# A two-layer encoder's norms: rows scaled by their inverse roots before they are transposed, or afterwards

## What is computed

```python
def rms_norm(x, g):
    xf = x.astype(jnp.float32)
    y = xf * lax.rsqrt(jnp.mean(xf * xf, axis=-1, keepdims=True) + EPS)
    return (y * g.astype(jnp.float32)).astype(x.dtype)

for layer in (even, odd):
    h = h + mixer(rms_norm(h, ln_mix[layer]))
    h = h + cross_attention(rms_norm(h, ln_cross[layer]), rms_norm(mem, ln_mem[layer]))
    h = h + hier_moe(rms_norm(h, ln_ffn[layer]))
out = rms_norm(h, ln_final)
```

## Time and profile before

| | |
|---|---|
| runs | 1172.38, 1172.42, 1177.09 us; median 1172.42 |
| span of the profiled execution | 1166.6 us; its own time with what lies around the span is not listed, the three runs stand for it |
| TensorE busy | 1073.4 us, 92% |
| VectorE, ScalarE busy | 274.1 us, 177.2 us |
| DMA | 284.09 MB, mean 244 GB/s |

### The profile page before, as it was taken

The page is one execution under the profiler, slowest core; times in us unless marked ns, Lnnn a source line. Parts: engine busy times, 40 slices in busy tenths (PEclk is TensorE's granted clock), DMA queues, the critical chain, the costliest instruction groups (busy, mean ns, idle before and its releaser), DMA issues.

```text
span 1166.6 us, 11120 instructions
## 1 busy us (share of the span) xinstructions
PE 1073.4 (92%) x4580; PEld 649.5 (56%) x4580; DVE 274.1 (23%) x676; ACT 177.2 (15%) x368; POOL 11.1 (1%) x21
## 2 busy tenths in 40 slices
PE   5998798999999999899999999997988799999996
PEld 4577367454444443478867777785464544444432
DVE  4125232341111111402121212122134311111114
ACT  2105202031111110111111111111021211111101
POOL 1020000000000000000000000000000000000000
PEclk9999899999999999899999999998999799999998
DMA  9855034229999999983491770953051099999992
GB/s 335 311 157 200 17 144 158 77 73 411 425 426 428 425 429 428 280 246 75 90 249 26 177 188 2 281 192 139 1 217 66 7 399 424 429 427 426 429 429 99
DMA packets 108231, 284.09 MB, mean 244 GB/s; under 512 B 3719, under 2 KB 81623, under 8 KB 95897
## 3 DMA queue, kind: packets, MB, share of 16 engines
q1 hardware_dynamic: 106736, 279.72, 64.8%
q0 software_dynamic: 1168, 3.40, 1.1%
q10 hardware_dynamic: 280, 0.31, 0.1%
HBM read 282.31 MB, written 1.11 MB: 243 GB/s over the span
## 4 chain that ended last, share of the span: by engine, by line
PE 88%; DVE 5%; DMA 4%; issue 2%; ACT 1%; DVEq 0%; SPq 0%; ACTq 0%
PE banks L928 81%; PE banks L1244 4%; DMA ring<-expert_w_up_in 3%; PE banks L931 2%; ACT scratch L676 1%; DMA scratch<-mem_in 1%; DVE scratch L1904 0%; DVE tmp L1489 0%; DVE nrm L1592 0%; DVE mx L1584 0%; ACT nrm L725 0%; DVE rst L1491 0%; DVE h L1503 0%; DVE nrm L1531 0%; DVE nrm L1606 0%
## 5 line engine op out<-in xcount | busy, mean ns | idle before, releaser
L928 PE MATMUL banks<-ring,scratch 128*64 128x512 f32 (+1 forms) x1760 | 433.9, 594 | 12.6 <-DMA ring<-expert_w_up_in 5.4
L928 PEld LDWEIGHTS banks<-ring,scratch 128*64 128x64 f32 (+1 forms) x1760 | 162.2, 144 | 274.0 <-issue 270.9
L928 PE MATMUL banks<-nT,ring 128*128 128x256 f32 x1104 | 240.7, 379 | 0.6 <-DVE scratch L604 0.6
L928 PEld LDWEIGHTS banks<-nT,ring 128*128 128x128 f32 x1104 | 209.7, 190 | 29.0 <-issue 1.2
L928 PE MATMUL banks<-ring,nT 128*128 128x384 f32 (+2 forms) x352 | 116.6, 487 | 0.0
L928 PEld LDWEIGHTS banks<-ring,nT 128*128 128x128 f32 x352 | 64.0, 191 | 44.7 <-issue 14.3
L928 PE MATMUL banks<-scratch 128*128 128x256 f32 (+4 forms) x292 | 67.2, 416 | 14.1 <-ACT scratch L676 10.0
L676 ACT ACTIVATE scratch<-banks 128x512 f32<-128x512 f32 (+1 forms) x84 | 47.5, 585 | 202.5 <-PE banks L928 112.1
L928 PEld LDWEIGHTS banks<-scratch 128*128 128x128 f32 (+2 forms) x292 | 49.3, 196 | 30.9 <-ACT scratch L676 14.7
L1511 DVE TENSOR_TENSOR h<-banks,h 128x512 f32<-128x512 f32 x56 | 38.8, 692 | 117.3 <-PE banks L1244 117.3
L928 PE MATMUL banks<-scratch,nrm 128*128 128x256 f32 x256 | 61.7, 398 | 2.4 <-issue 2.4
(11 more groups left out here) (146 smaller groups left out, 440.6 us busy)
## 6 DMA issues: line engine op xcount, KB each, us to landing
ring<-expert_w_gate_in SPq DMA_DIRECT2D x32, 2048.0 KB, 13.2
ring<-expert_w_up_in SPq DMA_DIRECT2D x32, 2048.0 KB, 14.2
ring<-expert_w_down_in SPq DMA_DIRECT2D x32, 2048.0 KB, 11.6
ring<-odd_w_in_in SPq DMA_DIRECT2D x72, 512.0 KB, 7.2
ring<-xkv_w_in SPq DMA_DIRECT2D x4, 2048.0 KB, 12.5
ring<-even_w_in_in SPq DMA_DIRECT2D x3, 2048.0 KB, 20.9
scratch<-bias_rows SPq DMA_DIRECT2D x8, 576.0 KB, 7.8
ring<-even_w_out_in SPq DMA_DIRECT2D x2, 2048.0 KB, 10.2
```

Of the source, the lines that this page charges most:

```text
L928: return giving_back(nc.tensor.matmul(dst, lhsT, rhs, start=start, stop=stop))
```

## The change

Raw rows are transposed with the identity as soon as they are there, one pass a piece and with no wait for a root. The evacuation multiplies by the gain as before. The inverse roots are kept for all norms (roots) and enter where the results are read:

- as a number per token on the partitions: values of the memory (v0a to v1b, odd values), the scale of cross attention's exponentials and of the negated maxima (scaled, negated), the odd logits, and the router's logits;
- as a row over the free dimension, "spread": TensorE multiplies ones with the two diagonals into a bank (spread), VectorE copies it to SBUF (rbc, or rbc1 in norm 1). Memory keys and odd keys are multiplied by rbc at their evacuation; norm 1 multiplies all its chunks by rbc1 and the gain at once, on VectorE alone.

With it go: k0b and k1b move from ScalarE to VectorE (BY_DVE); odd pieces go by kind, 1 and 2 to VectorE, 0, 3 and 4 to ScalarE; TensorE waits for the copies of the bias rows (vec_sb) before norm 1's spread; in norms 2, 3, 5 and 6 VectorE works out tile 1's root after its evacuations.

```diff
+        SPREAD = {"m": 0, "1": 1, "4": 2}
+        SCALED = {"2": 0, "5": 1, "4": 2}
...
-        def norm_source_ready(eng, name):
+        def norm_source_ready(eng, name, t=0):
...
-                piece_in(eng, "nm1")
             else:
-                eng.wait_ge(resid, AFTER[name] + 2)
+                eng.wait_ge(resid, AFTER[name] + 2 + 2 * t)
...
-                if (k % 2 == 1) != is_act:
+                if (name != "1" and k % 2 == 1) != is_act:
...
+                        if name == "1":
+                            last = nc.vector.scalar_tensor_tensor(out=dst[:, c, :], in0=src, scalar=gain[:, c:c + 1],
+                                                                  in1=rbc1, op0=ALU.mult, op1=ALU.mult)
...
+        BY_DVE = {"k0a", "k0b", "k1a", "k1b"}
 
         def by_act(name):
-            return name in BY_ACT or PIECES[name] % 2 == 1
+            return name in BY_ACT or (name not in BY_DVE and PIECES[name] % 2 == 1)
...
+        def evacuate_keys(eng, is_act, name, dst):
+
+            if is_act:
+                return
+            piece_in(eng, name)
+            nc.vector.tensor_tensor(dst, pbank(name).rearrange("p (b s) -> p b s", b=2),
+                                    rbc.unsqueeze(1).to_broadcast([P, 2, SEQ]),
+                                    ALU.mult).then_inc(evac[PIECES[name] % 2], 1)
...
-            if (k % 2 == 1) != is_act:
+            kind = m % 5
+            if (kind not in (1, 2)) != is_act:
                 return
...
             elif kind == 2:
-                last = put(ok[:, 1:3].rearrange("p g s -> p (g s)"), b[:, :])
+                last = nc.vector.tensor_tensor(ok[:, 1:3], b.rearrange("p (b s) -> p b s", b=2),
+                                               rbc.unsqueeze(1).to_broadcast([P, 2, SEQ]), ALU.mult)
...
                 for t in range(2):
                     last = nc.scalar.activation(prob[:, n, t, :], bank[n][:, t * 256:(t + 1) * 256], ACT.Exp,
-                                                bias=negm[:, n, t:t + 1], scale=float(P) ** -0.5,
+                                                bias=negm[:, n, t:t + 1], scale=scaled[:, l, t:t + 1],
...
             def norm(name):
-                i = NORM_SEQ[name]
                 for t in range(TILES):
-                    pe.wait_ge(diag_set, 2 * i + 1 + t)
+                    norm_source_ready(pe, name, t)
...
-                            last = mm(b[:, at:at + P], NORMS[name][0][:, t, c * P:(c + 1) * P], diag[:, t, :], True, True)
+                            last = flip(b[:, at:at + P], NORMS[name][0][:, t, c * P:(c + 1) * P])
...
+            def spread(name):
+
+                pe.wait_ge(diag_set, SPREAD[name] + 1)
+                for t in range(TILES):
+                    last = mm(spread_bank(name)[:, t * P:(t + 1) * P], ones, diag[:, t, :], True, True)
+                last.then_inc(rbc_ps, 1)
...
+            pe.wait_ge(id_in, 16)
             norm("m")
             keys(0, 0, "m")
+            spread("m")
             keys(0, 1)
...
+            pe.wait_ge(vec_sb, 1)
+            spread("1")
             norm("1")
...
-            for m in range(5):
+            head_piece(0, 0, 0)
+            spread("4")
+            for m in range(1, 5):
                 head_piece(m, 0, 0)
...
+                if name == "m":
+                    squares(0)
+                    squares(1)
+                    evacuate_norm(dve, False, name)
+                    both_roots()
+                    dve.wait_ge(id_in, 16)
+                    on_diagonal()
+                    spread_out(rbc)
+                elif name == "1":
+                    squares(0)
+                    squares(1)
+                    both_roots()
+                    middle()
+                    on_diagonal()
+                    spread_out(rbc1)
+                    evacuate_norm(dve, False, name)
+                elif name == "4":
+                    dve.wait_ge(resid, at + 4)
+                    evacuate_norm(dve, False, name)
+                    squares(1)
+                    both_roots()
+                    on_diagonal()
+                    scores_scales()
+                    spread_out(rbc)
                 else:
                     add(at, 0)
                     add(at, 1)
                     dve.wait_ge(ssq_act, i + 1)
                     variance(0)
-                    step(rsqrt([0]))
-                    on_diagonal(0)
+                    step(rsqrt(rst, [0]))
                     for f in range(2):
                         add(at, 2 + f)
                         dve.wait_ge(resid, at + 3 + f)
                         squares(f)
-                    step(v.tensor_tensor(ssq[:, 1:2], ssq[:, 1:2], ssq[:, 2:3], ALU.add))
+                    evacuate_norm(dve, False, name)
+                    step(v.tensor_tensor(sums[:, 1:2], sums[:, 1:2], sums[:, 2:3], ALU.add))
                     variance(1)
-                    rsqrt([1]).then_inc(rstd_set, 1)
+                    rsqrt(rst, [1]).then_inc(rstd_set, 1)
                     dve.wait_ge(rstd_set, i + 1)
-                    on_diagonal(1)
+                    if name in SCALED:
+                        scores_scales()
...
-                v.tensor_scalar(negm[:, n, :], mx[:, n, :], -float(P) ** -0.5, None, ALU.mult).then_inc(maxed, 1)
+                v.tensor_tensor(negm[:, n, :], mx[:, n, :], negated[:, a // X_HEADS, :], ALU.mult).then_inc(maxed, 1)
...
+                for t in range(TILES):
+                    last = v.scalar_tensor_tensor(out=lg[:, t], in0=pbank(k)[:, t * NR:(t + 1) * NR],
+                                                  scalar=root("36"[l], t), in1=rb[:, l], op0=ALU.mult, op1=ALU.add)
```

More of the change, by code:

```diff
@@ L577, in evacuate_filler @@
                 i = "ab".index(name[2])
-                evacuate(eng, is_act, name, two(xkT[:, 1, 2 * i:2 * i + 2]))
+                evacuate_keys(eng, is_act, name, xkT[:, 1, 2 * i:2 * i + 2])
             elif name in ("v1a", "v1b"):
-                evacuate(eng, is_act, name, xv[:, 1, "ab".index(name[2]), :])
+                t = "ab".index(name[2])
+                evacuate(eng, is_act, name, xv[:, 1, t, :], scale=root("m", t))
         def evacuate_norm(eng, is_act, name):
@@ L698, in rows_for_gathers @@
                                                 src[:, t, :].rearrange("p (q c) -> p q c", c=CH), ACT.Copy,
-                                                scale=rst[:, t:t + 1])
+                                                scale=root(name, t))
                 middle()
@@ new lines, in scores_scales @@
+                def scores_scales():
+                    n = SCALED[name]
+                    step(v.tensor_scalar(scaled[:, n, :], rst, float(P) ** -0.5, None, ALU.mult))
+                    if n < DEPTH:
+                        step(v.tensor_scalar(negated[:, n, :], rst, -float(P) ** -0.5, None, ALU.mult))
+                if name == "7":
+                    dve.wait_ge(resid, at + 4)
+                    squares(1)
+                    both_roots()
+                    dve.wait_ge(lnf_in, 16)
+                    for t in range(TILES):
+                        for f in range(2):
+                            cols = slice(f * 512, (f + 1) * 512)
+                            v.scalar_tensor_tensor(out=rows(t)[:, cols], in0=src[:, t, cols], scalar=rst[:, t:t + 1],
+                                                   in1=lnf[:, cols], op0=ALU.mult, op1=ALU.mult).then_inc(fin_set, 1)
+                    return
```

114 lines of the change are left out of this document (62 added, 52 removed).

## The result

| | before | after |
|---|---|---|
| median of four runs (lowest, highest) | 1172.4 us (1170.78, 1177.09) | 1178.84 us (1178.09, 1182.49) |
| profiled execution: own time, span | span 1166.6 | 1182.49, 1180.6 |

The ratio is 1.006, with a 95% interval of 1.0031 to 1.0089. A second comparison (first experiment) gave 1.0035 [1.0018, 1.0053]. By the medians the change costs 6.4 and 3.9 us, 0.35 to 0.6%; the forecast was 1173.1 us, +0.65. The time lies in the range and in its upper part; the first median is even above 1178.3, where the prediction's own "slower" begins, to which it had given 0.21. What carried it there is the subject of the rest.

The account below looks back on a forecast made before the run. TensorE was taken as the bound, busy 92% of the span and carrying 88% of the chain. Gains at norms 2 to 6 against losses elsewhere, chiefly +10.15 in the odd layer, summed to +0.65: 1173.1 us, range 1167 to 1180.

Parts of the forecast that it names:

- Norm 4: After the experts: transposes start straight behind the projection without waiting for roots and diagonals, first odd product earlier; -7.75 us.
- The branch: TensorE's jump over its second expert pass, now between projection and transposes: between 0 and 4.54 us, taken as 0.
- Norms 5 and 6: TensorE no longer waits for tile 1's diagonal; tile 1 is turned earlier; -3.1 and -2.95 us.
- Norms 2 and 3: Fillers already hide the roots; half of tile 0's records and a little of tile 1 go; -1.05 and -1.2 us.
- The memory norm: At the start: rows turned earlier, but key weights limit the gain and key products run on a cold clock; +1.0 us.
- Norm 1: TensorE waits for bias-row copies, diagonals and spread (+1.7), then value products run at half rate (+2.15); +3.8 us.
- the row that tells how TensorE recovers is the last odd head: Clock still 0.50 up to 818 us after transposes from 809.73, so 4.3 us of value products charged at half rate, +2.15.
- Cross attention 0: In layer 0, VectorE evacuates the second key filler ahead of normalising head 0, delaying its transposes; +1.75 us.
- The odd layer: Normalising waits for VectorE's piece 2 in all seven heads with a next head, not three; 4 x 2.54, +10.15 us.
- Rival A: Slower: the clock falls at three or four of norms 2, 4, 5 and 6; 1179.7 or 1181.9 us; chance 0.21.
- Rival B: Faster: odd-head normalising is ready in time, the 10.15 go, 1163 us; with unpaid cold stretches 1166.6 or less, chance 0.12.
- Rival C: A raw-row transpose takes as long as the diagonal pair; norms 2 to 6 give back about 3 us, 1176; chance 0.06.

Follow-up runs that it names:

- first experiment: The changed kernel with no edit, measured in more runs and profiled a second time: 1176.31 us (nine runs), ratio 1.0035 to the kernel before.
- again: The second profile of the unedited changed kernel, taken in the first experiment, whose median was 1176.31 us.
- the identity products: The changed kernel with norm transposes made as ordinary products with the identity: in all norms 1186.84 us, in norms m, 1, 2 and 3 only 1181.98 us.
- before with the order mended: The kernel before with VectorE normalising a head ahead of piece 2 of the next one, nothing else: 1166.52 us, 0.9932.
- the kernel with the order mended: The changed kernel with VectorE normalising a head ahead of piece 2 of the next one: 1158.18 us, 0.9878.

## Why the prediction came out as it did

**Norm 4, -7.75: right.** -8.11 to the first odd product, forecast -8.2 (the 0.45 of the spread is in the next segment). The branch, taken as 0 between 0 and 4.54, was 0 in the change by its place in the program; two variants with the same norm 4 paid 1.75 and 2.36 us there. That was luck: the reason given, that queued products cover it, held there as well.

**Norms 5 and 6, -3.1 and -2.95: right.** -3.12 and -2.87 in the profile after (-3.13 and -2.88 in "again"), and 0.5 us lost behind the second router.

**Norms 2 and 3, -1.05 and -1.2: right at the norms.** The records ahead of norm 2 come 9.12 us later than before, its first product 8.07 later; from cross attention 0 to the router it is -0.92 and -0.94. But the stretch behind that router takes 1.6 to 3.3 us longer in the change and in nearly all variants, with a clock of 0.50. The sum has no term for it. The version with 22 transposes in the wait for key weights had 10.60 there, like before; the three profiles of kernels with before's norms had 10.67 or 10.68. What decides it stays open: not transposes as such, as the identity products show.

**The memory norm, +1.0: right in kind, and it varies.** +1.7 and +0.5 in the two profiles of the change (start of keys -1.56 and -1.48, key products +3.28 and +1.97). The row on the cold norm is misread: 21 records in 4 us are 0.19 us each, two thirds of the rate of the earlier trace rows and not half.

**Norm 1, +3.8: mis-sized.** The way to the value product grew by 2.28, forecast 1.7. The value products, charged with 2.15 at half rate, lost 0.65 and 0.08: in the profile after the clock is 0.58 from 59.6 to 61.0 us and 1.00 from there on. So 2.4 to 2.9. The step that failed is "the row that tells how TensorE recovers is the last odd head": there it stood 6.25 us before it made transposes, here 3.05 us before four records of products and sixteen transposes, and the clock was back at 61.0 us, 5.9 us after TensorE went on at 55.15; behind the last odd head it was still 0.50 at 818, 8.3 us after 809.73. Nor is that row fixed: the twelve records of products behind the last head took 5.49 us in the profile of before and 2.86 with the clock at 1.00 in three other profiles, one of them of before with the order mended.

**Cross attention 0, +1.75: right**, 1.75 and 1.74. The three terms that it names add up to 1.47; where the rest comes from it doesn't say.

**The odd layer, +10.15: right in kind, too small by 2 to 5.** It was 12.9 and 15.8 with the spread's 0.45. Seven long heads came, by the mechanism and the 2.5 us named. What was missing: the wait is long enough for the clock to fall in some of them, and after the seventh that costs 1.3 in both profiles. The scale from memory, taken at 0 to 0.3 in the last head, fits: TensorE waits 6.38 us there instead of 6.25. The prediction used "waits of 2.05 and 2.37 us are today followed by full rate" from two single rows; three such waits in one execution can't say how seven will do.

**Rival A** foresaw the loss by clock but in the wrong places. Behind norms 2, 4 and 5 and in the first 3 us behind norm 6 the profile after shows a clock of 1.00; the falls were in the odd heads' waits and at the router, and transposes hold the clock up. Its figure, 1179.7, is nearer to the first median than the forecast is; the mechanism at the norms is not what gave it. **Rival B** is refuted by the change, and is nearly the kernel with the order mended. **Rival C** falls: 16 transposes take 2.04 us at norm 4, 0.13 each, and a piece as a diagonal product takes 2.05/8 = 0.26.

So the sum of +0.65 moves up by clock falls in the odd layer (2.3 to 5.2) and at the router (1.6 to 3.3) and down by some 1.2 at norm 1: +3.3 to +8, around the measured 3.9 and 6.4. That it came out so near zero at first is the cancelling of 16 us won against 17 lost, and a miss of 5 in the odd layer shows in full. The first expert stage, from its gathering products (246.75 us before, 258.92 after) to the end of its projection, has no term in the sum. It took 238.5 us before, 238.9 after and 242.1 in "again"; 1.7 of the last is a fall at those first products (8.83 us instead of 7.14). What the rest is stays open.

## What to carry to other kernels

When a change redistributes work among engines, write out each receiving engine's program and look for what now stands ahead of the thing the bottleneck waits for: one line cost 11.8 us, another order of the same instructions won 18.1. Compare a profile with the spread of its runs before taking differences of spans. In this kernel a wait of 2.3 us on TensorE cost its length and, in two to four of seven, 1.0 to 1.7 us more behind it. Where a change and its side effects come together, as inverse roots and pieces by kind here, cost them separately: the idea was worth 6 to 8 us (2 to 11 by the intervals), the assignment that came with it -12.

## What the runs showed of the hardware

- Under a stream of nothing but float32 transposes TensorE's rate rose from 6 to 11 records a microsecond and stayed up: the key products behind 44 of them took 7.07 us, behind 5.36 us of idling 9.98.
- The same jump in TensorE's program cost nothing or left 0.95 to 1.8 us of issue behind the last addition; the kernels differ in how much stands ahead of it in the program.
- In or right behind the router's products of layer 0 the clock fell to 0.50 in ten of eleven profiles of the change and its variants (12.3 to 13.9 us instead of 10.6 to 10.7), and in none of three with the norms of before.
- Unchanged code of the even mixer took 103.99 to 108.50 us in three profiles, and the same norm 1 7.20 or 8.83.
